# A mixture-of-experts kernel without a last stage: every expert block gathers its rows' sums, adds, normalises and scatters

## The chip, the cores and the metric

The kernel runs on one core of a Trainium2 chip. The metric is the device time of one execution in microseconds (us). The names of the engines: PE is TensorE, with its weight loads as PEld, DVE is VectorE, ACT is ScalarE, POOL is GpSimd, SP is SyncE. DMAs issued by an engine's queue are written SPq or ACTq; those of POOL are rows of POOL itself.

## The reference

One layer of a streaming encoder. After attention and a recurrence, every token (2048 of a prompt, 128 of running streams) goes through two of 32 SwiGLU experts, the result is added to its residual row, and the row is normalised:

```
t = rmsnorm(y, norm2_w)                      # 2176 rows of 1024
experts, gates = router(t)                   # 2 of 32 experts for each token
# rows sorted by expert, in blocks of 128 rows of one expert
for each block:  ys = (silu(xb @ wg[e]) * (xb @ wu[e])) @ wd[e]      # 1024 -> 512 -> 1024
y = y + segment_sum(ys * gate, row_token)    # each token gets two rows
y_prompt, y_sample = rmsnorm(y, final_w)
```

All of it is float32. The other outputs (keys, values, states) are written by earlier stages and are not touched.

## The kernel before

The program is a row of stages, each closed by a barrier of all engines: `project`, `attend_sample`, `attend_mix`, `experts`, `finish`. When `experts` starts, DRAM holds `h2` (the normalised rows) and `y` (the residual rows), and SBUF holds lists of which token each row of each block is.

`experts` works on 45 blocks of 128 rows, block b with expert `run_of(b)`. Some experts have one block and some have two (a run of blocks). There is no scheduler: each engine has its own program, the order of which is written out by hand, and semaphores tie them. For block b:

- **SP** loads the three weight matrices of an expert (2 MB each) into one of two slots, as soon as the block that used the slot last is through with it.
- **POOL** gathers the 128 token rows (`gather`, four indirect DMAs, 3 blocks ahead), the gates (`gate_of`), and at the end scatters the block's result (`scatter`): an indirect DMA that adds `block_out` to the rows of `scratch_y` in DRAM. Two scatters must not overlap, since two blocks can hold the same token, so each waits for the one before it (`o_out`).
- **PE** runs `gate_up(b)` (`gate_psum` L1968, `up_psum` L1972) and then `down(b - 1)` (`down_psum` L1983), 16 matmuls of 128x512 each.
- **ACT** takes exp of the gate (L1867), then issues 16 small DMAs (`spread_a`, L1874) that lay `hidden` out for the transpose, then empties the first half of `down_psum` of the block before (`copy_out`, L1880).
- **DVE** runs, in this order: `hidden(b)` (L1911 to L1917), `turn_x(b + 1)` (L1906), `copy_out(b - 1)` (the other half of `down_psum`, L1929), `turn_a(b)` (the transpose that makes `hidden_T`, L1922, once the 16 DMAs have landed). `down(b)` needs `hidden_T`, and `gate_up(b + 1)` needs `turn_x(b + 1)` and `hidden(b)`.

`finish` then loads the 17 tiles of `scratch_y` by SP, takes the mean square on ACT (L2047 to L2049), scales on DVE (L2057), and stores the tiles into two output tensors. The first load of `finish` can start only after the last scatter has landed and the barrier is past.

## Time and profile before

| | |
|---|---|
| median of 3 runs | 2894.78 us (2892.29 to 2896.38) |
| the profiled execution | 2889.87 us, span 2888.1 us |
| PE busy in the span | 2686.8 us (93%) |
| DVE, ACT, POOL busy | 1494.0 us (52%), 720.3 us (25%), 664.2 us (23%) |
| expert blocks | from about 1877 us to 2823 us |
| from the last `down_psum` to the end of the span | 2823.1 us to 2888.1 us |
| bytes moved by DMA | 404.42 MB |

The span runs from the first to the last recorded event; the device time is 1.8 us longer. PE is busy nearly all the time up to the last expert block, and not at all in `finish`.

### The profile page before, as it was taken

To read this page: it belongs to the slowest core of one execution; us is meant where nothing else is said; L and a number is where in the kernel's file an instruction comes from. 1 tells how busy PE (TensorE), PEld (TensorE's weight loads), DVE (VectorE), ACT (ScalarE), POOL (GpSimd) and SP (SyncE) were. 2 spreads that over 40 slices of the span, in tenths; PEclk is the share of its full clock that TensorE was granted. 3 is DMA by queue.
4 is the path that set the end of the run, shared out by engine and by line. 5 is a ranking of instruction groups with operands and counts; after the bars stand their busy time and mean duration, and the time that the engine had idled before them with its cause. 6 is when DMAs were issued, how large, how long until landed. Compare 5 with 4: busy or idle time off the path is not lost. (4 is left out here: it accounts for less than half of the span.)

```text
span 2888.1 us, 38265 instructions
## 1 busy us (share of the span) xinstructions
PE 2686.8 (93%) x11801; PEld 1617.9 (56%) x11802; DVE 1494.0 (52%) x2787; ACT 720.3 (25%) x2014; POOL 664.2 (23%) x921
## 2 busy tenths in 40 slices
PE   8999999999999986999999999499999999999990
PEld 6777777777777765555555555244444444444430
DVE  2565655556655564676777775434343434343333
ACT  1222222122222213555556664000000000000004
POOL 2111111111111111112222222223233333333330
PEclk9999999999999997999999999599999999999995
DMA  6010001000010046322121212299888688886877
GB/s 249 31 36 26 25 25 40 29 33 25 25 36 33 26 135 239 117 88 79 53 88 45 66 63 78 77 374 308 299 266 279 198 280 277 288 278 211 268 236 269
DMA packets 225977, 404.42 MB, mean 140 GB/s; under 512 B 30866, under 2 KB 88594, under 8 KB 225888
## 3 DMA queue, kind: packets, MB, share of 16 engines
q1 hardware_dynamic: 172976, 342.30, 33.4%
q0 software_dynamic: 18208, 48.64, 6.7%
q10 hardware_dynamic: 34704, 12.37, 1.7%
q8 instruction: 46, 0.75, 0.1%
q14 instruction: 43, 0.35, 0.0%
HBM read 310.62 MB, written 80.79 MB: 136 GB/s over the span
## 5 line engine op out<-in xcount | busy, mean ns | idle before, releaser
L670 PE MATMUL z_psum<-w_in_sb,hT 128*128 128x512 f32 x1088 | 480.5, 592 | 0.0
L664 PE MATMUL z_psum<-hT,w_in_sb 128*128 128x128 f32 x3264 | 375.2, 276 | 3.0 <-DMA w_in_sb<-in_w_in 3.0
L664 PEld LDWEIGHTS z_psum<-hT,w_in_sb 128*128 128x128 f32 x3264 | 371.0, 193 | 3.8 <-issue 3.8
L1968 PE MATMUL gate_psum<-w_gate_sb,block_rows_T 128*128 x720 | 321.4, 600 | 20.4 <-DMA w_gate_sb<-in_w_e_gate 20.4
L1983 PE MATMUL down_psum<-w_down_sb,hidden_T 128*128 x720 | 318.2, 595 | 7.1 <-DVE hidden_T L1922 7.1
L670 PEld LDWEIGHTS z_psum<-w_in_sb,hT 128*128 128x128 f32 x1088 | 200.5, 190 | 221.0 <-issue 221.0
L1972 PE MATMUL up_psum<-w_up_sb,block_rows_T 128*128 x720 | 316.3, 592 | 0.0
L1636 PE MATMUL y_psum<-w_out_sb,mix_T 128*128 128x512 f32 x512 | 239.7, 612 | 11.2 <-DVE mix_T L1391 11.2
L1265 ACT ACTIVATE w_in_sb<-score_psum,neg_max 128x512 f32<-128x512 f32 (+3 forms) x320 | 196.8, 622 | 209.5 <-DVE neg_max L1352 209.3
L1968 PEld LDWEIGHTS gate_psum<-w_gate_sb,block_rows_T 128*128 128x128 f32 x720 | 138.5, 193 | 195.9 <-issue 195.9
L1983 PEld LDWEIGHTS down_psum<-w_down_sb,hidden_T 128*128 128x128 f32 x720 | 137.4, 191 | 180.8 <-issue 180.8
L310 POOL TENSOR_TENSOR level_decay<-log_decay 128x256 f32<-128x256 f32 x116 | 73.5, 634 | 704.4 <-DVE level_operand L505 704.4
L1972 PEld LDWEIGHTS up_psum<-w_up_sb,block_rows_T 128*128 128x128 f32 x720 | 136.8, 190 | 172.2 <-issue 172.2
L1880 ACT ACTIVATE block_out<-down_psum,block_gates 128x512 f32<-128x512 f32 x45 | 30.9, 687 | 805.3 <-issue 795.0
L1215 POOL TENSOR_SCALAR w_in_sb<-w_in_sb,seg_factor,map_coef 128x512 f32<-128x512 f32 (+3 forms) x160 | 112.2, 711 | 493.5 <-DVE seg_factor L1365 493.5
L1352 DVE TENSOR_REDUCE neg_max<-score_psum 128x2 f32<-128x1024 f32 (+3 forms) x160 | 170.1, 1063 | 91.8 <-PE score_psum L1599 88.8
L1922 DVE STREAM_TRANSPOSE hidden_T<-hidden_by_lane 128x512 f32<-128x512 f32 x45 | 32.0, 711 | 348.3 <-DMA hidden_by_lane<-hidden 348.3
L1816 POOL DMA_INDIRECT block_rows<-scratch_h,block_tokens x188 | 179.4, 954 | 80.4 <-issue 41.1
L1834 POOL DMA_INDIRECT scratch_y<-block_out,block_out_rows x45 | 73.5, 1634 | 496.6 <-ACT block_out L1880 492.3
L1636 PEld LDWEIGHTS y_psum<-w_out_sb,mix_T 128*128 128x128 f32 x512 | 93.6, 192 | 149.2 <-issue 126.5
L1618 PEld LDWEIGHTS att_out_psum<-w_in_sb,weights_T 128*128 128x128 f32 x1088 | 133.5, 192 | 72.8 <-issue 61.0
L520 DVE COPY_PREDICATED scores_T<-level_mask,level_psum 128x512 f32<-128x512 uint8 x133 | 97.5, 733 | 146.8 <-PE level_psum L685 146.8
(295 smaller groups left out, 3389.7 us busy)
## 6 DMA issues: line engine op xcount, KB each, us to landing
w_gate_sb<-in_w_e_gate SPq DMA_DIRECT2D x32, 2048.0 KB, 13.8
w_up_sb<-in_w_e_up SPq DMA_DIRECT2D x32, 2048.0 KB, 13.3
w_down_sb<-in_w_e_down SPq DMA_DIRECT2D x32, 2048.0 KB, 15.0
w_in_sb<-in_w_in SPq DMA_DIRECT2D x7, 2048.0 KB, 19.1
hidden_by_lane<-hidden ACTq DMA_DIRECT2D x720, 16.0 KB
scratch_z<-z_ring SPq DMA_DIRECT2D x34, 256.0 KB, 2.0
scratch_y<-w_in_sb SPq DMA_DIRECT2D x17, 512.0 KB, 2.6
scratch_h<-h SPq DMA_DIRECT2D x17, 512.0 KB, 2.6
```

Source lines behind the costliest of these rows:

```text
L520: ins = nc.vector.copy_predicated(heads(A[:, :]), mk, heads(lps[pos % 2][:, :]))
L664: mm = pe.matmul(out[:, hd * P:(hd + 1) * P], w[:, g, c, hd * P:(hd + 1) * P], hT[:, u, c, :], start=(c == 0), stop=(c == DC - 1))
L670: mm = pe.matmul(out[:, :], hT[:, u, c, :], w[:, g, c, :], start=(c == 0), stop=(c == DC - 1))
L1215: pool.tensor_scalar(w1, w1, fac[:, u % 2, 1, s:s + 1], coef[:, 1:2], ALU.mult, ALU.mult).then_inc(w1_ok, 1)
L1265: ins = nc.scalar.activation(pr, sps[n % 2][:, c, 0:kw * P], ACT.Exp, bias=nmax[:, u % 2, c, s:s + 1], accum_out=zsum[:, u % 2, c, s:s + 1])
L1352: red(nmax[:, u % 2, :, s:s + 1], sps[n % 2][:, :, 0:kw * P], AX.X, ALU.max, negate=True).then_inc(m_ok, 1)
L1618: mm = pe.matmul(ops[:, 0:P], wT[:, n % 2, b * P:(b + 1) * P], v[:, k0 + b, head(u)], start=(s == 0 and b == 0), stop=(s == count(u) - 1 a ...
L1636: mm = pe.matmul(bank(m, part)[:, :], mT[:, m % 2, c, :], wo[:, c, part * HW:(part + 1) * HW], start=(c == 0), stop=(c == DC - 1))
L1816: pool.indirect_dma_start(out=xg[:, u, i, :], out_offset=None, in_=dr["h2"].rearrange("t (j d) -> (t j) d", j=LANES), in_offset=bass.Indir ...
L1968: mm = pe.matmul(gps[:, :], xT[:, u, c, :], part(wg, slot, c), start=(c == 0), stop=(c == DC - 1))
L1972: mm = pe.matmul(ups[:, :], xT[:, u, c, :], part(wu, slot, c), start=(c == 0), stop=(c == DC - 1))
L1983: mm = pe.matmul(dps[:, half, :], aT[:, u, c, :], part(wd, slot, c, slice(half * HW, (half + 1) * HW)), start=(c == 0), stop=(c == FC - 1))
```

## The change

`finish` is gone. `experts` now makes the sums and the finished rows itself:

- POOL: `sums(b)` gathers the block's rows of `scratch_y` into `block_sums`, after the scatter of the block before has landed. `scatter(b)` writes the new sums back as a plain write, without adding. `final(b)` scatters the normalised rows into a new output array `out_y_all`, that holds the prompt's rows, the streams' rows and 128 rows of padding, and is cut in two by views on the host. A token's row is written twice, and the second write, which holds the full sum, stays. The last block has no `scatter` and no `gate_of`.
- DVE: `copy_out` becomes `add` (two instructions, one for each half of `down_psum`, that scale by the gate and add `block_sums`), and `final` (one instruction over 1024 columns) comes after `turn_a`.
- ACT: `copy_out` is gone. `stats` takes the mean square of the sums and its root's inverse, after `spread_a`. A load of the activation table stands at the head of the loop's body, which is two blocks long, and ahead of and behind the loop.
- PE: the matmuls are the same; `down` waits for `add` where it waited for the two copies.

```diff
-            def scatter(b, u):
+            def sums(b, u, finals):
                 wait(pool, o_out, 16 * b)
+                wait(pool, f_out[u], 16 * finals)
                 pool.tensor_copy(dest[:, u:u + 1], col(tok_all, b)).then_inc(dest_ok, 1)
                 pool.wait_ge(dest_ok, b + 1)
-                pool.wait_ge(d_act, b + 1)
-                pool.wait_ge(d_dve, b + 1)
+                pool.sem_inc(stand, 1)
+                pool.indirect_dma_start(out=yg[:, u, :], out_offset=None, in_=dr["y"],
+                                        in_offset=bass.IndirectOffsetOnAxis(ap=dest[:, u:u + 1], axis=0)).then_inc(y_in, 16)
+            def scatter(b, u):
+                pool.wait_ge(s_ok, b + 1)
                 pool.sem_inc(stand, 1)
                 pool.indirect_dma_start(out=dr["y"], out_offset=bass.IndirectOffsetOnAxis(ap=dest[:, u:u + 1], axis=0),
-                                        in_=out[:, u, :], in_offset=None, compute_op=ALU.add).then_inc(o_out, 16)
+                                        in_=out[:, u, :], in_offset=None).then_inc(o_out, 16)
                 gate_of(b + 2, u)
+            def final(b, u, finals):
+                pool.wait_ge(f_ok, b + 2)
+                wait(pool, f_out[1 - u], 16 * finals)
+                pool.sem_inc(stand, 1)
+                pool.indirect_dma_start(out=dr["y_all"], out_offset=bass.IndirectOffsetOnAxis(ap=dest[:, u:u + 1], axis=0),
+                                        in_=fo[:, u, :], in_offset=None).then_inc(f_out[u], 16)
...
             with pool.Fori(1, n) as i:
                 gather(i * 2 + 3, 1)
+                sums(i * 2, 0, i)
+                final(i * 2 - 1, 1, i)
                 scatter(i * 2, 0)
                 gather(i * 2 + 4, 0)
+                sums(i * 2 + 1, 1, i)
+                final(i * 2, 0, i)
                 scatter(i * 2 + 1, 1)
-            scatter(n * 2, 0)
+            sums(n * 2, 0, n)
+            final(n * 2 - 1, 1, n)
+            final(n * 2, 0, n)
...
-            def copy_out(b, u):
...
-                nc.scalar.activation(out[:, u, 0:HW], dps[:, 0, :], ACT.Copy, scale=gcol[:, u:u + 1]).then_inc(d_act, 1)
+            def stats(b, u):
+                act.wait_ge(s_ok, b + 1)
+                wait(act, f_ok, b)
+                chain.after(nc.scalar.activation(junk[:, :], out[:, u, :], ACT.Square, accum_out=st[:, u, 0:1]))
+                chain.after(nc.scalar.activation(st[:, u, 1:2], st[:, u, 0:1], ACT.Ln, scale=1.0 / D, bias=consts["eps"][:, 0:1]))
+                nc.scalar.activation(st[:, u, 2:3], st[:, u, 1:2], ACT.Exp, scale=-0.5).then_inc(r_ok, 1)
...
             with act.Fori(1, n) as i:
+                nc.scalar.preload_act_table_set(ACT_SET)
                 blk(i * 2 + 1, 1)
...
-                ts(out[:, u, HW:D], dps[:, 1, :], gcol[:, u:u + 1], None, ALU.mult).then_inc(d_dve, 1)
+            def add(b, u):
                 dve.wait_ge(d_ps, b + 2)
...
+                dve.wait_ge(y_in, 16 * b + 16)
+                wait(dve, r_ok, b)
+                for half in range(2):
+                    c = slice(half * HW, (half + 1) * HW)
+                    ins = nc.vector.scalar_tensor_tensor(out=out[:, u, c], in0=dps[:, half, :], scalar=gcol[:, u:u + 1], in1=yg[:, u, c],
+                                                         op0=ALU.mult, op1=ALU.add)
+                ins.then_inc(s_ok, 1)
+            def final(b, u, finals):
+                dve.wait_ge(r_ok, b + 2)
+                wait(dve, f_out[u], 16 * finals)
+                nc.vector.scalar_tensor_tensor(out=fo[:, u, :], in0=out[:, u, :], scalar=st[:, u, 2:3], in1=fw[:, :],
+                                               op0=ALU.mult, op1=ALU.mult).then_inc(f_ok, 1)
...
                 hidden(b)
                 turn_x(b + 1, 1 - u)
-                copy_out(b - 1, 1 - u)
+                add(b - 1, 1 - u)
                 turn_a(b, u)
+                final(b - 1, 1 - u, finals)
...
-def finish(nc, dr, consts):
```

How this moves instructions: on DVE, the first of the two blocks in the loop's body, from the transpose of the gathered rows to the gate's first step of the next block, in the kernel before:

```order
L1906 STREAM_TRANSPOSE block_rows_T<-block_rows 128x1024
L90 REGISTER_ALU
L1928 ISA
L1929 TENSOR_SCALAR block_out<-down_psum,block_gates 128x512
L1920 REGISTER_ALU
L1922 STREAM_TRANSPOSE hidden_T<-hidden_by_lane 128x512
L1911 TENSOR_SCALAR silu_gate<-silu_gate 128x512
```

and in the changed kernel:

```order
L1944 STREAM_TRANSPOSE block_rows_T<-block_rows 128x1024
L1965 ISA
L1966 ISA
L1970 SCALAR_TENSOR_TENSOR block_out<-down_psum,block_gates,block_sums 128x512 x2
L1958 REGISTER_ALU
L1960 STREAM_TRANSPOSE hidden_T<-hidden_by_lane 128x512
L90 REGISTER_ALU
L1979 SCALAR_TENSOR_TENSOR block_final<-block_out,final_stats,final_row 128x1024
L1949 TENSOR_SCALAR silu_gate<-silu_gate 128x512
```

The one instruction over `down_psum` became two, and a third stands between the transpose of `hidden_by_lane` and the next block's `hidden`.

On POOL, one block in the loop's body, from the gathers of token rows to the gates, before:

```order
L1812 COPY block_tokens<-block_rows_all 128x4
L1813 REGISTER_ALU
L1816 DMA block_rows<-scratch_h,block_tokens 128x256 x4
L90 REGISTER_ALU
L1829 ISA
L1829 COPY block_out_rows<-block_tokens_all 128x1
L1834 DMA scratch_y<-block_out,block_out_rows 2304x1024
L1820 REGISTER_ALU
L1820 COPY block_slots<-block_slots_all 128x1
L1823 DMA block_gates<-scratch_gates,block_slots 128x1
```

and now:

```order
L1817 COPY block_tokens<-block_rows_all 128x4
L1818 REGISTER_ALU
L1821 DMA block_rows<-scratch_h,block_tokens 128x256 x4
L90 REGISTER_ALU
L1835 ISA
L1835 COPY block_out_rows<-block_tokens_all 128x1
L1838 DMA block_sums<-scratch_y,block_out_rows 128x1024
L1852 DMA out_y_all<-block_final,block_out_rows 2304x1024
L1844 DMA scratch_y<-block_out,block_out_rows 2304x1024
L1825 REGISTER_ALU
L1825 COPY block_slots<-block_slots_all 128x1
L1828 DMA block_gates<-scratch_gates,block_slots 128x1
```

Two indirect DMAs were put ahead of the scatter: the gather of this block's sums and the scatter of the finished rows of the block before.

## Rows read from the trace of the kernel before

**Rows 1.** Windows: stretch, us, busy PE, PEld, DVE, ACT, POOL, PEclk, DMA share, GB/s.

```profile
1900.00:2823.00 923.00, 915.90 (x2126) 404.71 (x2125) 339.10 (x309) 56.28 (x88) 307.30 (x391) 0.99 0.83 270
2840.00:2888.10 48.10, 0.00 (x0) 0.00 (x0) 21.66 (x17) 28.29 (x69) 0.00 (x0) 0.50 0.96 382
```

**Rows 2.** Waits, 1870 to 2830 us: who waited for whom: us, times, longest.

```profile
PE down_psum L1983 <- DVE hidden_T L1922: 7.1, 1, 7.1
POOL block_out_rows L1829 <- DMA scratch_y<-block_out,block_out_rows: 19.5, 14, 3.2
```

**Rows 3.** Timeline of a block with weights in flight: start, us, engine, line, what.

```profile
2033.86 0.71 DVE L1922 STREAM_TRANSPOSE hidden_T<-hidden_by_lane 128x512 f32<-128x512 f32 x1 [8.60 <-DMA hidden_by_lane<-hidden]
...
2037.89 7.03 PE L1983 MATMUL down_psum<-w_down_sb,hidden_T 128*128 x16
...
2039.21 0.69 DVE L1917 TENSOR_TENSOR hidden<-up_psum,silu_gate 128x512 f32<-128x512 f32 x1 [0.22 <-DVE silu_gate L1913]
2039.82 1.23 DVE L1906 STREAM_TRANSPOSE block_rows_T<-block_rows 128x1024 f32<-128x1024 f32 x1
2039.94 10.14 ACTq L1874 DMA_DIRECT2D hidden_by_lane<-hidden  x16
...
2044.76 7.03 PE L1968 MATMUL gate_psum<-w_gate_sb,block_rows_T 128*128 x16
...
2054.80 0.71 DVE L1922 STREAM_TRANSPOSE hidden_T<-hidden_by_lane 128x512 f32<-128x512 f32 x1 [8.90 <-DMA hidden_by_lane<-hidden]
...
2058.49 7.03 PE L1983 MATMUL down_psum<-w_down_sb,hidden_T 128*128 x16
```

**Rows 4.** Timeline of the stage's first down, and of a block whose weights are there.

```profile
1921.15 7.03 PE L1968 MATMUL gate_psum<-w_gate_sb,block_rows_T 128*128 x16
...
1932.00 0.71 DVE L1922 STREAM_TRANSPOSE hidden_T<-hidden_by_lane 128x512 f32<-128x512 f32 x1 [9.89 <-DMA hidden_by_lane<-hidden]
...
2321.59 0.71 DVE L1922 STREAM_TRANSPOSE hidden_T<-hidden_by_lane 128x512 f32<-128x512 f32 x1 [7.92 <-DMA hidden_by_lane<-hidden]
...
2327.67 10.14 ACTq L1874 DMA_DIRECT2D hidden_by_lane<-hidden  x16
...
2339.04 0.71 DVE L1922 STREAM_TRANSPOSE hidden_T<-hidden_by_lane 128x512 f32<-128x512 f32 x1 [4.74 <-DMA hidden_by_lane<-hidden]
```

**Rows 5.** Windows one block wide, of each kind (columns as in rows 1).

```profile
2032.10:2052.70 20.60, 20.60 (x49) 9.12 (x48) 7.66 (x7) 1.28 (x2) 6.62 (x10) 1.00 1.05 359
...
2320.50:2341.10 20.60, 20.60 (x49) 9.12 (x48) 8.63 (x9) 1.28 (x2) 6.80 (x9) 1.00 0.40 115
```

**Rows 6.** Timeline of POOL: two scatters, and the next copy of row numbers.

```profile
2093.70 1.62 POOL L1834 DMA_INDIRECT scratch_y<-block_out,block_out_rows  x1 [11.48 <-ACT block_out L1880]
...
2104.73 0.18 POOL L1829 COPY block_out_rows<-block_tokens_all 128x1 uint32 x1 [1.69 <-DMA scratch_y<-block_out,block_out_rows]
...
2813.79 1.63 POOL L1834 DMA_INDIRECT scratch_y<-block_out,block_out_rows  x1 [10.61 <-ACT block_out L1880]
...
2820.54 0.18 POOL L1829 COPY block_out_rows<-block_tokens_all 128x1 uint32 x1 [3.15 <-DMA scratch_y<-block_out,block_out_rows]
```

**Rows 7.** Timeline of the last block and of the last stage.

```profile
2813.36 0.71 DVE L1922 STREAM_TRANSPOSE hidden_T<-hidden_by_lane 128x512 f32<-128x512 f32 x1 [5.29 <-DMA hidden_by_lane<-hidden]
...
2823.35 0.75 DVE L1929 TENSOR_SCALAR block_out<-down_psum,block_gates 128x512 f32<-128x512 f32 x1 [9.28 <-PE down_psum L1983]
2825.01 1.61 POOL L1834 DMA_INDIRECT scratch_y<-block_out,block_out_rows  x1 [4.29 <-DVE block_out L1929]
...
2840.42 1.28 ACT L2044 ACT_TABLE_LOAD   x1 [16.41 <-PEq L72]
2845.69 1.06 ACT L2047 ACTIVATE square_out<-y_final 128x1024 bf16<-128x1024 f32 x1 [4.00 <-DMA y_final<-scratch_y]
...
2847.53 1.28 DVE L2057 SCALAR_TENSOR_TENSOR y_out<-y_final,final_stats,final_row 128x1024 f32<-128x1024 f32 x1 [23.43 <-ACT final_stats L2049]
...
2883.71 0.33 SPq L2034 DMA_DIRECT2D out_y_sample<-y_out  x1
```

More of the change, by code:

```diff
@@ L1842, in _ @@
             gather(2, 0)
+            sums(0, 0, 0)
             gather(3, 1)
@@ L1845, in _ @@
             gather(4, 0)
+            sums(1, 1, 0)
+            final(0, 0, 0)
             scatter(1, 1)
@@ L1861, in _ @@
             n = load(act, trips[0:1, 0:1], 1, MAXT)
+            chain = Chain(act, act_step)
             def gate(b):
```

106 lines of the change are left out of this document (35 added, 71 removed).

## The prediction, made before the changed kernel was run

> **What bounds the kernel now.** I read the windows first, to see which engine has no room. Over the expert blocks PE is busy 915.9 of 923 us at a granted clock of 0.99, and in the last stage it has nothing to do, while the DMA moves 382 GB/s for 48.1 us [rows 1]. So there are two limits. In the expert stage it is PE: one block is 2058.49 - 2037.89 = 20.60 us from `down` to `down` [rows 3]. In the last stage it is the DMA. Then the waits: `down` waits once for `hidden_T`, 7.1 us [rows 2], at the last block. The question is what disappears behind the last `down`, and whether anything added to DVE, ACT, POOL and the DMA breaks the cover that PE gives.
>
> The third view is the timeline of one block, read as a ring. DVE makes `hidden`, ACT issues 16 DMAs, they land, DVE transposes them to `hidden_T`, and only then does DVE start the next `hidden`. With weights in flight one transpose starts 2054.80 - 2033.86 = 20.94 us after the other [rows 3]: 5.35 to L1917, 0.73 to the first issue, 10.14 of issues, 4.72 of landing. Where the weights are there already, the landing is 2339.04 - 2337.81 = 1.2 us and the step 17.45 us [rows 4]. So **a second ring, of nearly PE's length, lies right behind PE's**: 0.3 us slower than PE in a loaded block, 3.2 faster in a quiet one. Of the 45 windows of one block between 1867 and 2794 us I count 14 with a DMA share of 0.39 to 0.70, the others at 0.96 to 1.05, as the two of [rows 5]: 14 quiet blocks, and behind the first one 29 loaded steps.
>
> Where the ring stands against PE is one number, x: the start of `hidden_T` counted from the end of the `down` before it, which is the start of the `gate_psum` matmuls. In the loaded block of [rows 3] x is 2054.80 - 2044.76 = 10.0 us.
>
> **What goes.** The last `down` is read at 2823.35 and the span ends at 2888.1 [rows 7]: 64.75 us. In the changed kernel this tail is as follows. `add` is two instructions; for one half there are 0.75 (from PSUM) and 0.64 (half of L2057's 1.28), and I take 0.72, so 1.45 us. 0.1 to ACT. From the start of L2047 to the start of L2057, 2847.53 - 2845.69 = 1.84. The scaling, 1.28. Then POOL picks it up after 0.91 (from DVE's end at 2824.10 to 2825.01) [rows 7], and the scatter lands 6.75 us after its issue, as the one at 2813.79 did, with no weights in flight [rows 6]. With the start at 2823.35 the sum ends at 2835.7, if `down` ends when it does now. **Gain 52.4 us.** Bounds of the landing: at most 4.4 us, for a plain store issued at 2883.71 [rows 7], and 11.03 us, for a scatter beside weights [rows 6]: gain 48 to 55. The sums of the last block must be there in time; their gather starts when scatter 43 has landed, which by 6.75 us is some 6 us ahead of the last `down`'s end. I count it as hidden.
>
> **What comes, engine by engine.**
>
> PE: nothing. `down` waits for `add`, which ends some 1.6 us after the `down` before it and is needed 13.7 us after it (two thirds of 20.60).
>
> ACT loses its copy and gets `stats`, 1.8 us, and at the head of each second block a table load of 1.28 [rows 7]. Its DMA issues are out at x - 4.7 in a loaded block, so the next exp can start at x - 1.6, ahead of DVE, which comes for it at x + 2.0. In a quiet block it starts at x + 1.9, about half a us late, in at most 4 of the 14: 2 us, left out. The Trainium skill (ScalarE: Activation LUTs, What ACT_TABLE_LOAD costs) puts a drain of about 1.38 us behind the load at a switch to another set; with it those 4 blocks would cost some 6 us more. The trace shows the load alone, 1.28, and the set here is the one in use.
>
> DVE: `add` costs 0.7 us more than the copy, at a place where DVE waits 4.7 us and more for the DMAs [rows 3, 4]: hidden. **`final`, 1.28 and 0.02 to start, is not hidden.** It stands between the transpose and the next `hidden`, inside the ring. A loaded step becomes 20.94 + 1.30 = 22.24, 1.64 over PE's 20.60, and a quiet one 17.45 + 1.30 = 18.75, 1.85 under it.
>
> The ring meets PE where PE needs `turn_x(b + 1)`: it ends 5.35 + 1.30 + 0.61 + 1.23 = 8.5 us after the start of the transpose, and PE comes for it at 20.6, so the limit is x = 12.1. (`down` itself would wait from x = 13.0.) The first block of the stage has x = 1932.00 - 1921.15 = 10.9 [rows 4], so the limit is reached in the next step. From there each loaded step over the limit is lost to PE, and a quiet one gives 1.85 of room. The room never gets so large that x would fall to where PE holds it now, so the account is one line: 29 x 1.64 = 47.6, less 14 x 1.85 = 25.9, plus what x has fallen at the end, 10.9 - 10.25 = 0.7: **22.4 us lost**. The last block pays once more: its `down` has no `gate_up` ahead of it and waits for `hidden_T`. There x is 6.2 now (5.29 of idle time [rows 7], behind a copy that takes 0.75 and starts 0.2 after `down`), and 10.25 then: 4.0 us. **Loss 26.4 us.**
>
> The ends of this term: with a landing 0.5 us shorter in loaded blocks it is 29 x 0.5 less, 12; with one 0.5 longer, 41. I stay with the landing of today's rows, which is that of the same DMAs beside the same weights.
>
> POOL gets two more indirect DMAs of 1.62 for each block. It waits 10.6 and 11.5 us ahead of a scatter today [rows 6], so its time is covered. New is a **chain through DRAM**: scatter(b - 1), its landing, sums(b), its landing, add(b), scatter(b). From a scatter to the next copy of row numbers POOL needs 11.03 - 1.69 = 9.34 us for its own work [rows 6]; then 1.0 to the gather's issue, g for its landing, 0.1 to DVE, 1.45 for `add`, 0.9 to POOL: 12.8 + g. The trace has no gather of this size. The bounds for g are 6.75 and 11.03 us, both of adding scatters of the same rows [rows 6]: 19.5 to 23.8 us against PE's 20.6. Only 14 of 45 scatters landed later than 9.34 us [rows 2], so I take 8: 20.8 us, on a par with PE and shorter than the ring. And `add` can be some 5 us late before the transpose behind it is.
>
> DMA: a loaded block moves 359 GB/s x 20.6 us = 7.4 MB [rows 5]. Two transfers of 0.52 MB more make 8.4, less what the adding scatter read. At the 382 GB/s of the last stage [rows 1] that takes 22.1 us, about the ring's 22.2: it doesn't add to it, but it says that loaded blocks stay loaded.
>
> **Sum.** Gain 52.4, loss 26.4, net 26.0 us. The profiled execution, 2889.87 us, becomes 2863.9; it is 4.9 us below the median of the runs, so the median of 2894.78 becomes 2868.8. Forecast **2869 us**.
>
> **Rivals.**
>
> 1. *The ring keeps its room.* The landing shrinks, since a plain scatter is shorter than an adding one, or since the weights come at a slower pace with PE. Then the loss is 0 to 12 us, and the time 2894.8 - 52.4 + 6 = 2848. For it: the term hangs on 1.64 us a step, of which half a us of landing takes a third. Against it: in the loaded blocks the DMA share is 1.05 [rows 5], with nothing to spare.
>
> 2. *The quiet blocks stop being quiet.* With x near 12 the last of the 16 DMAs in a quiet block is issued about 9 us after `down`, close to where the next expert's weights may start. Then a quiet step gives nothing back, or even costs what a loaded one does: 47.6 us, up to 47.6 + 14 x 1.64 = 71, and 4 at the end. Time 2894 to 2917; I take 2900, slower or the same. For it: the landing goes from 1.2 to 4.7 us when weights are in flight [rows 3, 4]. The Trainium skill (DMA: Bandwidth & Descriptors, Queues, rings and completion order) says that a DMA engine goes from one queue to the next only after a whole packet of some 9 to 17 descriptors; by that rule the new gathers and scatters would lengthen this landing as well, and the time would be that of this rival. No row here shows such a transfer beside the 16 small ones.
>
> 3. *The chain through DRAM becomes the bound*, place: DVE's wait for the sums. With g at 11.03 in 30 blocks and 6.75 in the others it costs 30 x 3.2 - 14 x 1.1 = 81 us: 2894.8 - 52.4 + 81 = 2923, slower than before. It decides from 44 x (12.8 + g - 20.6) > 52.4, a mean g over 9.0 us. For it: the 11.03. Against it: that was an adding scatter, and most were under 9.34.
>
> 4. *The tail doesn't shrink as it should*, since the close of the program has a cost of its own. The span holds 4.4 us behind the last store [rows 7], and the device time 1.8 behind the span: some us at most, inside the range.
>
> **Chances.** Forecast (loss 12 to 45, so 2854 to 2887): 0.50. Rival 1: 0.22. Rival 2: 0.13. Rival 3: 0.15. A measurement of this kernel tells about 0.2%, 5.8 us. Faster by more than that: 0.50 + 0.22 + 0.03 = 0.75. Within it: 0.10, out of rivals 2 and 3. Slower: 0.15. The range goes from a loss of 4 us, 2846, into rival 2, 2897; 0.05 is left out below and 0.15 above.
>
> **What would show it.** In the profile after: a span that ends 12 to 13 us behind the last `down`, with no SPq rows there. In the expert stage PE waits, 1 to 2 us each, for `block_rows_T` or `hidden_T` by DVE, in the rows of loaded blocks and not around quiet ones, and from `hidden_T` to `hidden_T` it is 22.2 us there. If DVE's `add` waits 5 us and more for the gathered sums, it is rival 3; if the distance is 22 us also where the weights are there, rival 2; if PE has no waits, rival 1. I am wrong altogether if PE's waits name `add`, or the weights.

## The result

The changed kernel is slower: 2927.43 us (median of 4 runs, 2922.29 to 2932.77) against 2895.58 before (4 runs, beside it on the same chip), a ratio of 1.0111 with a 95% interval of 1.009 to 1.0133. Forecast were 2869 us and a range from 2846 to 2897. The profiled execution took 2929.27 us, its span 2927.5.

The medians differ by 32 us, the two profiled executions by 39.4: the one before lies 5.7 under its median, this one 1.8 over. Sums from the traces, here and below, are to be set against the 39.4. The first fence holds the timeline of the changed kernel from the last `down` to the end (start, us, engine, line, what, idle time before it):

```profile
2912.01 1.41 DVE L1970 SCALAR_TENSOR_TENSOR block_out<-down_psum,block_gates,block_sums 128x512 f32<-128x512 f32 x2 [8.57 <-PE down_psum L2036]
2913.45 1.06 ACT L1909 ACTIVATE square_out<-block_out 128x1024 bf16<-128x1024 f32 x1 [11.56 <-DVE block_out L1970]
...
2915.29 1.28 DVE L1979 SCALAR_TENSOR_TENSOR block_final<-block_out,final_stats,final_row 128x1024 f32<-128x1024 f32 x1 [1.87 <-ACT final_stats L1911]
2917.44 0.96 POOL L1852 DMA_INDIRECT out_y_all<-block_final,block_out_rows  x1 [12.14 <-DVE block_final L1979]
```

The last stage is gone: 2927.5 - 2912.01 = 15.5 us are left of the 64.75 of [rows 7], a gain of 49.3. But the last `down` is read at 2912.01, not at 2823.35: **the expert stage is 88.7 us longer** (88.7 - 49.3 = 39.4). Its waits in the changed kernel (1870 to 2925 us; who waited for whom: us, times, longest), which answer to [rows 2]:

```profile
DVE hidden_T L1960 <- DMA hidden_by_lane<-hidden: 558.5, 45, 15.9
PE down_psum L2036 <- DVE hidden_T L1960: 55.7, 29, 13.0
PE gate_psum L2022 <- DVE block_rows_T L1944: 32.6, 31, 16.7
DVE block_out L1970 <- DMA block_sums<-scratch_y,block_out_rows: 0.4, 1, 0.4
```

PE waits 55.7 us for the transpose that ends the ring, once 7.1 us before, and 32.6 for `turn_x`, which comes behind the ring's `hidden`; 16.7 of these are the start of the stage. The gathered sums are waited for once, 0.4 us. Windows of the same 800 us, before and then after (columns as in [rows 1]):

```profile
1900.00:2700.00 800.00, 800.00 (x1861) 353.96 (x1861) 299.22 (x272) 49.18 (x77) 268.70 (x342) 1.00 0.84 276
```

```profile
1900.00:2700.00 800.00, 752.82 (x1709) 323.10 (x1709) 329.29 (x314) 99.87 (x193) 290.57 (x384) 0.99 0.84 302
```

PE had no idle time and now has 47 us. The granted clock is nearly the same, and the DMA engines are no busier than before (0.84), though they move more. The page's chain of work that ended last is the ring's through this stage:

```profile
ACTq 14%; DVE 9%; DMA 9%; issue 2%; PE 1%; DVEq 0%; SPq 0%; POOL 0%; ACT 0%; POOLq 0%
ACTq L1903 14%; DMA hidden_by_lane<-hidden 8%; DVE silu_gate L1950 5%; DVE block_final L1979 2%; DMA w_gate_sb<-in_w_e_gate 1%; DVE hidden L1955 1%; DVE silu_gate L1951 1%; DVE silu_gate L1949 1%; PE down_psum L2036 0%; PE gate_psum L2022 0
```

**The ring in three terms.** From the starts of the rows of `hidden` and `hidden_T` in all 45 blocks I worked out for each run: r, from the transpose `hidden_T` to the next `hidden`; 10.87, which is 0.73 to the first issue and 10.14 of 16 issues [rows 3]; and the landing, what then is left to the next transpose. Their sum is the step by construction, in every run, so it proves nothing by agreeing; it says which part of the step grew. Where DVE waits for PE, that wait lies in r. Since 10.87 is held fixed, a train of issues that takes longer than 10.14 us counts as landing (in the mean it took 10.17 before and 10.32 after). Before, the mean landing is 3.66 us, 14 of 45 are under 2 us (the quiet blocks), and the step is PE's, 20.51. After:

6.54 + 10.87 + 5.15 = 22.56 us, against a mean step of 22.53 (45 landings, 44 steps).

44 steps of 2.02 us more are 89, the stage's whole loss. With the landing of before it would be 6.54 + 10.87 + 3.66 = 21.07, and 44 x 0.56 = 25 us. So `final` in the ring is some 25 us, near the forecast, and **64 us come from a landing that is 1.5 us longer: no landing is under 2 us any more**.

**Which landings.** Set beside the same block of the kernel before, 59 of the 64 us lie in its 14 quiet blocks, where the mean landing rose from 1.23 to 5.45 us. In the other 31 it went from 4.83 to 5.00.

Why, the trace shows in such a block, the 32nd. Its rows before, and then after (timeline):

```profile
2533.80 10.14 ACTq L1874 DMA_DIRECT2D hidden_by_lane<-hidden  x16
2539.15 7.03 PE L1968 MATMUL gate_psum<-w_gate_sb,block_rows_T 128*128 x16
2545.17 0.71 DVE L1922 STREAM_TRANSPOSE hidden_T<-hidden_by_lane 128x512 f32<-128x512 f32 x1 [4.87 <-DMA hidden_by_lane<-hidden]
2546.60 0.39 SPq L1778 DMA_DIRECT2D w_gate_sb<-in_w_e_gate  x1
```

```profile
2595.54 10.44 ACTq L1903 DMA_DIRECT2D hidden_by_lane<-hidden  x16
2597.66 7.03 PE L2022 MATMUL gate_psum<-w_gate_sb,block_rows_T 128*128 x16
2605.11 0.39 SPq L1783 DMA_DIRECT2D w_gate_sb<-in_w_e_gate  x1
2611.24 0.71 DVE L1960 STREAM_TRANSPOSE hidden_T<-hidden_by_lane 128x512 f32<-128x512 f32 x1 [11.71 <-DMA hidden_by_lane<-hidden]
```

SP's fetch of the next expert's `w_gate` waits for PE's last use of that slot, so it follows the block's `gate_psum`: 7.45 us behind their start in both kernels. The 16 small issues follow the ring. Before, they ended 4.8 us behind the start of `gate_psum`, and the weights came 2.7 us later, when all had landed. Now they end 8.3 us behind it, and **the weights are issued 0.9 us ahead of the last small transfer**. The queues' packets from 2606 to 2611.2 us there (queue, packets, MB, share of the engines), q1 the weights, q0 GpSimd's, q10 the 16 transfers:

```profile
q1 hardware_dynamic: 631, 1.29, 75.6%
q0 software_dynamic: 85, 0.25, 19.1%
q10 hardware_dynamic: 96, 0.03, 2.4%
```

It is the same in all 13 quiet blocks that have a fetch behind them (the 14th is the last block): in the changed kernel the weights are 0.4 to 1.7 us ahead of the last small issue and the landings, from its end on, 4.0 to 6.3 us; before, the weights were 0.1 us ahead in one block and 1.4 to 2.8 behind in 12, and every landing was 1.2 to 1.3.

It feeds itself. While PE has its own pace the 16 issues of a quiet block end early. Once PE waits for `turn_x`, `gate_psum` starts just behind it, and the last issue ends 10.87 us behind the start of `hidden`, less the 0.61 and 1.23 up to the end of `turn_x`: 9.0 us behind the start of `gate_psum` (measured, 7.9 to 9.2), past the 7.45 of the weights. So a ring that makes PE wait also takes from itself the quiet landings in which it would catch up.

GpSimd's transfers lie on some landings too. In the block before that one, which had weights in flight before the change (landing 4.8 us), the weights are now through early, and from 2584 to 2588.3 us there is this:

```profile
q0 software_dynamic: 250, 0.63, 44.8%
q10 hardware_dynamic: 448, 0.15, 13.5%
q1 hardware_dynamic: 8, 0.02, 1.2%
```

The landing is 2588.27 - 2585.84 = 2.4 us. In the quiet block of [rows 4], 2335 to 2339 us of the kernel before, the same view has one queue only, and the landing is 1.2 us:

```profile
q10 hardware_dynamic: 288, 0.10, 10.3%
```

The gathers are there because the change brings them forward without moving their lines. The timeline of GpSimd in that block of the changed kernel; its 16 issues began at 2575.70 and ended at 2585.84:

```profile
2578.93 0.96 POOL L1844 DMA_INDIRECT scratch_y<-block_out,block_out_rows  x1 [6.77 <-DVE block_out L1970]
...
2586.71 0.94 POOL L1821 DMA_INDIRECT block_rows<-scratch_h,block_tokens  x1 [0.30 <-issue]
```

Before, these gathers stood behind a scatter that waited for ScalarE's half of the copy, and ScalarE reached it behind its 16 issues: in one block ScalarE issued from 2595.94, copied at 2606.27, and GpSimd scattered at 2607.76. The change took ScalarE's half away, GpSimd waits for VectorE's `add` alone, and the whole of its work for the block goes out some 8 us earlier (3.2 us behind the first of the 16 issues here, 11.8 there), under the 16 transfers. So three things could make the ring long enough for PE to wait: 1.28 us in it, 1 MB a block more on the queues, and this move. The runs try them one by one.

### The profile page after: what moved, and what is told of

Same layout as the page of the kernel before. It is cut to its first block and busy times, and to the rows that moved or that the text cites. A ratio compares the mean times of both kernels' runs of the same rounds, so it can differ in the third digit from the quotient of the medians.

```text
span 2927.5 us, 38632 instructions
## 1 busy us (share of the span) xinstructions
PE 2707.5 (92%) x11801; PEld 1615.3 (55%) x11802; DVE 1551.8 (53%) x2860; ACT 763.6 (26%) x2103; POOL 718.7 (25%) x1008
## 5 line engine op out<-in xcount | busy, mean ns | idle before, releaser
L2036 PE MATMUL down_psum<-w_down_sb,hidden_T 128*128 x720 | 328.2, 610 | 55.7 <-DVE hidden_T L1960 55.7
L2022 PE MATMUL gate_psum<-w_gate_sb,block_rows_T 128*128 x720 | 323.6, 603 | 38.0 <-DVE block_rows_T L1944 32.6
L1909 ACT ACTIVATE square_out<-block_out 128x1024 bf16<-128x1024 f32 x45 | 47.5, 1057 | 873.7 <-issue 862.2
L1599 PE MATMUL score_psum<-w_in_sb,att_q 64*128 64x512 f32 (+3 forms) x640 | 162.2, 585 | 1.6 <-PEq L72 1.5
```

Source lines behind the costliest of these rows:

```text
L1599: mm = pe.matmul(sps[n % 2][:, c, 0:kw * P], q[r, p % 2, head(u)], k[r, k0:k0 + kw, head(u)], start=True, stop=True)
L2022: mm = pe.matmul(gps[:, :], xT[:, u, c, :], part(wg, slot, c), start=(c == 0), stop=(c == DC - 1))
L2036: mm = pe.matmul(dps[:, half, :], aT[:, u, c, :], part(wd, slot, c, slice(half * HW, (half + 1) * HW)), start=(c == 0), stop=(c == FC - 1))
```

## The experiments

Ratios are against the kernel before, on the same chip, with 95% intervals. Landing and step are means worked out as above; PE's pace is 20.5. "Overtaken" counts, of the 13 quiet blocks of the kernel before with a fetch behind them, those in which the weights are issued 0.4 us or more ahead of the last of the 16.

| run | us | ratio | r | landing | under 2 us | overtaken | step |
|---|---|---|---|---|---|---|---|
| before | 2895.58 | 1 | 6.00 | 3.66 | 14 | 0 | 20.51 |
| changed | 2927.43 | 1.0111 | 6.54 | 5.15 | 0 | 13 | 22.53 |
| e1_final_off_ring | 2889.45 | 0.9987 | 5.37 | 5.43 | 0 | 9 | 21.67 |
| e2_ring_alone | 2922.02 | 1.0104 | 6.55 | 3.85 | 11 | 6 | 21.25 |
| e3_dmas_alone | 2926.86 | 1.0111 | 5.35 | 5.12 | 1 | 12 | 21.34 |
| e4_ring_and_dmas | 2972.68 | 1.0274 | 6.55 | 5.02 | 1 | 13 | 22.41 |
| e6_gather_alone | 2895.18 | 1.001 | 5.94 | 3.73 | 13 | 0 | 20.52 |
| e7_scatter_alone | 2887.24 | 0.998 | 5.89 | 3.78 | 14 | 0 | 20.53 |
| e11_two_gathers | 2937.05 | 1.0146 | 5.36 | 5.30 | 1 | 12 | 21.53 |
| e14_dve_copies_both | 2943.03 | 1.0168 | 5.36 | 5.49 | 0 | 8 | 21.71 |
| e5_silu_ahead | 2845.76 | 0.984 | 1.33 | - | - | 0 | 20.57 |

In e5 the transpose does not wait for the landing, so there is none to read. Counted from the last issue itself, 5 landings of e14 are 1.7 to 2.0 us: its 16 issues took 10.5 us in the mean.

The last column but one orders what follows. Over the 15 kernels that leave the hidden row's steps in their place, these are 195 blocks. In the 130 that are overtaken the landing, from the last issue on, is 3.7 to 6.8 us. In the other 65 it is 1.2 to 3.6, but for two: the first quiet block of e3 and of e11, with 5.5 and 6.6 us. No run holds the weights back and changes nothing else, so this is read from the traces of all these edits, and was not tried by hand.

**First: ring, transfers, both.** e1_final_off_ring moves `final` in the changed kernel to where VectorE waits anyway:

```diff
                 turn_x(b + 1, 1 - u)
...
+                final(b - 2, u)
                 add(b - 1, 1 - u)
                 turn_a(b, u)
-                final(b - 1, 1 - u, finals)
...
```

> The changed kernel with one instruction moved: DVE's final(b - 1) no longer stands between the transpose of block b and the hidden of block b + 1, but one block later, behind turn_x(b + 2) and ahead of add(b), where DVE waits for the 16 DMAs. All DMAs stay. Theory A (the 1.28 us inside the ring is what breaks the cover, and the longer landings follow from the lateness that it causes): the step from hidden_T to hidden_T falls to at most 20.9 us, PE's waits in the stage go under 10 us, and the time is 2895.6 less the tail's gain of some 49, so 2845 to 2860. Theory B (the new gathers and scatters lengthen the landing of the 16 DMAs by themselves, from 4.7 to over 6 us): the step is the 22.55 us of the changed kernel less 1.24, 21.3, over PE's 20.6, and the time is 2870 to 2885.

Measured: 2889.45 us, ratio 0.9987 (0.9977 to 0.9997), 38 us under the changed kernel. r fell by 1.17, the landing stayed long (9 of 13 overtaken), and PE still waits 47.6 us for `hidden_T`. The place of `final` matters, and is not all. Both theories missed: the time lies 4 us over B's range and far over A's.

e2_ring_alone is the kernel before with a spare instruction of the size of `final` at its place:

```diff
                 copy_out(b - 1, 1 - u)
                 turn_a(b, u)
+                spare()
...
```

> The kernel before, with one more DVE instruction of 1024 columns (1.28 us, on tiles that nothing else uses) between turn_a(b) and hidden(b + 1), and no other change; the last stage is still there. Theory A, as in the forecast's account: 22.4 + 4.0 = 26 us over before, 2922, with a loaded landing of 4.7 us and a quiet one of 1.2. If lateness alone turns the quiet blocks loaded: 50 to 75 over before. Theory B: 26 at most, as the DMAs are unchanged.

Measured: 2922.02 us, 1.0104 (1.0085 to 1.0123), 28 us. The landing hardly changes in the mean, and 11 are under 2 us. But they are not the same 11: in 6 of the 13 quiet blocks the weights are 0.4 to 1.3 us ahead and the landing is 3.7 to 5.5 us, in the other 7 they are at most 0.2 ahead and it is 1.2 to 1.3, and 3 of the 11 lie in blocks that were loaded before, where the weights are through early. So lateness alone does overtake, here in half of the blocks. The 26 us of the account came out, but not by its terms: it had all quiet landings at 1.2.

e3_dmas_alone is the kernel before with both transfers of the change as spare ones:

```diff
                 pool.wait_ge(dest_ok, b + 1)
...
+                pool.indirect_dma_start(out=yg[:, u, :], in_=dr["y"], ...).then_inc(y_in, 16)
...
+                pool.indirect_dma_start(out=dr["spare"], in_=go[:, :], ...).then_inc(f_out, 16)
+                pool.wait_ge(y_in, 16 * b + 16)
                 pool.wait_ge(d_act, b + 1)
```

> The kernel before, with two more indirect DMAs on POOL for each block, of the size and at the place of those in the changed kernel: a gather of the block's rows of scratch_y and a plain scatter of a spare tile into a spare array. Neither is used; DVE, ACT and PE are as before. Theory A: the loaded landing rises by less than 0.4 us, and the time is within 6 us of before. Theory B: the loaded landing is 6 us and more, the loaded step over 22 us, and the time 20 to 45 us over before.

Measured: 2926.86 us, 1.0111 (1.0091 to 1.013), 33 us, theory B's time with a shorter landing than its 6 us. All of it is in the landing, and 12 of 13 blocks are overtaken. The first quiet block has a landing of 5.5 us with the weights only 0.1 us ahead, where the kernel before has 1.3: there the added transfers themselves lengthen it. The DMA engines are at 0.94, with PE at 781 of 800 us:

```profile
1900.00:2700.00 800.00, 781.29 (x1798) 339.27 (x1797) 283.49 (x259) 43.66 (x75) 325.25 (x396) 1.00 0.94 314
```

e4_ring_and_dmas has both additions.

> Both additions at once: the spare DVE instruction in the ring and the two spare DMAs for each block, on the kernel before. If the two causes only add, the loss is that of the two runs before together; if they amplify each other, it is more than the sum. For the changed kernel's loss in the expert stage, 88 us, both theories together need 80 to 90 us here, so 2975 to 2985.

Measured: 2972.68 us, 1.0274 (1.0256 to 1.0293), 79 us, 2 under the lower end expected, and more than 28 + 33. Alone, each has to use up first what the ring lacks to PE's pace: by the means of the table it is 5.36 + 10.87 + 3.66 = 19.9 us without waits for PE, 0.6 under 20.5 (an estimate). 79 less the tail's 49 is 30, near the changed kernel's 32.

**Second: which transfer?** e6_gather_alone and e7_scatter_alone are e3 with only one of its two transfers.

> The kernel before, with one more transfer a block: a gather of the block's 128 rows of the sums into a spare array (its content is not used), issued and landed before the block's scatter. Both spare transfers together cost 33 us (e3_dmas_alone). If any 0.5 MB a block beside the hidden row's 16 transfers lengthens their landing: 12 to 20 us, mean landing 4.3 to 4.6 us, about 2906 to 2914. If only a write (the plain scatter) does it, because it goes out where the loaded and the quiet blocks' transfers start: under 6 us here, and 27 and more in e7_scatter_alone. If the gather does it, since GpSimd now also waits for it before the scatter and so everything behind it is issued later: 25 us and more here.

> The kernel before, with one more transfer a block: a plain scatter of 128 rows of zeros into a spare array (read by nothing), issued just before the block's own scatter. If any 0.5 MB a block does it: 12 to 20 us, mean landing 4.3 to 4.6 us, about 2906 to 2914. If the write alone does it: 27 us and more (over 2920). If the gather alone does it: under 6 us.

Measured: e6 2895.18 us, 1.001 (0.9992 to 1.0027); e7 2887.24, 0.998 (0.9971 to 0.999). Each alone is free, with 13 and 14 quiet landings and no block overtaken. No theory on record fits both numbers. The ten runs of e6 spread over 19 us, from 2885.58 to 2904.96, and its trace is of one at the lower end, 2887.86: whether some of its runs were overtaken isn't known. e11_two_gathers asks if it takes a read and a write:

```diff
                 pool.indirect_dma_start(out=yg[:, u, :], in_=dr["y"], ...).then_inc(y_in, 16)
+                pool.indirect_dma_start(out=yh[:, u, :], in_=dr["y"], ...).then_inc(y_in, 16)
-                pool.wait_ge(y_in, 16 * b + 16)
+                pool.wait_ge(y_in, 32 * b + 32)
```

> The kernel before with two spare gathers of the block's sums, one behind the other, ahead of the block's scatter: the same 1 MB a block as in e3_dmas_alone, but reads only. If the amount decides (0.5 MB more a block still leaves pauses of the weights under the 16 transfers, 1 MB more leaves none): 20 to 40 us slower, mean landing near 5 us. If it needs a gather and a plain scatter together (a read and a write at once): within 8 us of the kernel before, 12 and more landings under 2 us.

Measured: 2937.05 us, 1.0146 (1.0129 to 1.0163), 41 us, one landing under 2 us, 12 of 13 overtaken. So **half a MB a block more is free here and a whole one is not**, with reads alone too. The edit has a second effect: GpSimd's scatter waits 258.2 us for the two gathers (28 times; 83.1 in e6 and 3.0 in e3), so what is behind it goes out later, and amount and place are not cleanly apart in it. The DMA shares over the same 800 us are 0.84 before, 0.91 with one gather and 0.94 with two.

Then the same question in the changed kernel: e9_no_final_scatter leaves the scatter of the finished rows out, e10_no_gather the gather of the sums (each block adds to zeros).

> The changed kernel without the scatter of the finished rows (the y outputs are not written), 0.5 MB a block less; the sums are gathered, added to, normalised and scattered as in the changed kernel. So far, beside the kernel before: gather alone +1, plain scatter alone -7, both together +33, the ring's 1.28 us alone +28, all of it +79. Theory A (the landing of the hidden row's 16 transfers lengthens from 3.7 to 5.1 us only when the queues carry both added transfers, as these four runs say; with one of them the pauses of the weights still meet the 16 transfers): the landing falls to 3.7 to 4.2 us, the step of the ring from 22.5 to 21.3, the time from 2927 to 2865 to 2885 (of it some 3 us at the end, where nothing lands after the last scatter of a finished row). Theory B (in the changed kernel it is where the transfers stand, the gather of the sums or the scatter under the 16 transfers, and not their number): one of e9 and e10_no_gather stays above 2910 and the other falls by 40 and more.

> The changed kernel without the gather of the sums (each block adds to zeros, so the sums and outputs are not the reference's), 0.5 MB a block less. Theory A: as e9_no_final_scatter, 2870 to 2890. Theory B: see there. Theory C (the path through DRAM from a block's sums scattered to the next block's gather costs time although the profile shows 0.4 us of waits for it): the gain here is larger than in e9_no_final_scatter by 10 us and more.

Measured: e9 2915.41 us, 1.0076 (1.0059 to 1.0093); e10 2920.37, 1.0077 (1.0059 to 1.0095); only 12 and 7 us under the changed kernel where 40 and more were expected, with landings of 4.72 and 5.01 us. By their ratios the two are alike. All theories missed. What keeps the landings long is the place of the weights: with `final` still in the ring PE still waits for it, and 10 and 11 of the 13 blocks are overtaken. In e9 the others have landings of 1.2 to 2.2 us. Nor does the path through DRAM cost anything that shows: e10 has none and gains no more than e9.

**Third: the place of GpSimd's work.** e14_dve_copies_both makes, in the kernel before, only the move of GpSimd's work:

```diff
@@ VectorE, copy_out
+                ts(out[:, u, 0:HW], dps[:, 0, :], gcol[:, u:u + 1], None, ALU.mult)
                 ts(out[:, u, HW:D], dps[:, 1, :], gcol[:, u:u + 1], None, ALU.mult).then_inc(d_dve, 1)
@@ ScalarE, copy_out: left out; GpSimd and TensorE no longer wait for it
-                pool.wait_ge(d_act, b + 1)
```

> The kernel before, with ScalarE's half of `copy_out` done on VectorE, behind its own half: nothing is added to the transfers and nothing to the ring (the copy stands ahead of turn_a, where VectorE waits for the landing anyway), but GpSimd's scatter and the gathers behind it no longer wait for ScalarE, whose copy stood behind the 16 transfers, and go out some 8 us earlier, under the landing. This is the move that the changed kernel made without a line of the diff naming it. Theory P: 15 to 35 us slower, under 5 landings below 2 us, GpSimd's queue at some 0.3 of the engines in the landing. Theory R: within 5 us of the kernel before.

Measured: 2943.03 us, 1.0168 (1.015 to 1.0186): **50 us for an edit that adds no byte and nothing to the ring**, more than theory P had allowed. The landing of the 31 loaded blocks rose from 4.83 to 5.67 us, the gathers being on it, and 8 of 13 quiet blocks are overtaken; in the other 5 it is 2.7 to 3.6. The timelines of GpSimd and of ScalarE in it, one block:

```profile
2619.20 1.63 POOL L1833 DMA_INDIRECT scratch_y<-block_out,block_out_rows  x1 [11.23 <-DVE block_out L1921]
...
2623.79 0.98 POOL L1816 DMA_INDIRECT block_rows<-scratch_h,block_tokens  x1 [0.79 <-POOL block_tokens L1812]
...
2627.58 0.94 POOL L1816 DMA_INDIRECT block_rows<-scratch_h,block_tokens  x1 [0.30 <-issue]
```

```profile
2614.71 10.60 ACTq L1873 DMA_DIRECT2D hidden_by_lane<-hidden  x16
```

and VectorE's transpose behind them:

```profile
2631.24 0.71 DVE L1913 STREAM_TRANSPOSE hidden_T<-hidden_by_lane 128x512 f32<-128x512 f32 x1 [12.86 <-DMA hidden_by_lane<-hidden]
```

The four gathers are issued from 2623.79 to 2628.52, around the end of the 16 issues at 2625.31, and the landing takes 5.9 us. PE waits 51.2 us for `hidden_T`, 30 times.

e13_scatter_late tries to undo the move in the changed kernel, e15_final_off_ring_late in e1 and e16_no_final_late in e9, all with one line:

```diff
             def scatter(b, u):
                 pool.wait_ge(s_ok, b + 1)
+                pool.wait_ge(r_ok, b + 2)
...
```

> The changed kernel, with one more wait: GpSimd's scatter of a block's sums also waits for ScalarE's `stats` of the block, which stands behind the 16 transfers on ScalarE's queue, as ScalarE's copy did in the kernel before. So the scatter, the gate's gather and the four gathers of rows behind it go out some 8 us later, as they did before, and no longer while the 16 transfers land. Theory P (place: in the changed kernel these gathers were moved under the landing; place, amount and ring each end the quiet landings, and together they cost little more than two of them): since ring and amount alone cost 79 us beside the kernel before (e4_ring_and_dmas) and the changed stage 88, 5 to 12 us faster than the changed kernel, 2915 to 2923. Theory Q (the place is the main part of the 88 us): 2900 or less. Theory R (the place does nothing): 2925 to 2930. The gather of the next block's sums is late here and may add some us of waits of `add`, which is not in the ring.

> e1_final_off_ring (2889) with the late scatter of e13_scatter_late: of the three costs only the amount is left, 33 us (e3_dmas_alone), less the tail's 49. Theory P: 2875 to 2882, 8 to 14 us under e1_final_off_ring. Theory R: as e1_final_off_ring, 2887 to 2892.

> e9_no_final_scatter (the finished rows are not scattered; 2915) with the late scatter of e13_scatter_late. Of the added transfers only the gather is left, which cost nothing in e6_gather_alone, and the place is as in the kernel before, so of the three costs only the ring's 28 us is left, less the tail's 49. Theory P: 2870 to 2885, quiet landings are back (over 8 under 2 us). Theory R (removing one transfer bought 12 us in e9 for another reason): 2905 and more.

Measured: e13 2923.95 us (1.0111, 1.0095 to 1.0128), e15 2897.43 (1.0017, 1.0007 to 1.0026), e16 2906.97 (1.0043, 1.0028 to 1.0057). e13 can't be told from the changed kernel (the same ratio), e15 is 8 us slower than e1, e16 8 us faster than e9. e15 missed both its theories, e16's time is that of R, with 4 landings under 2 us, and e13 lies between P and R. The waits of e13 show that this is no clean undoing:

```profile
DVE block_out L1971 <- DMA block_sums<-scratch_y,block_out_rows: 318.7, 44, 10.0
DVE hidden_T L1961 <- DMA hidden_by_lane<-hidden: 254.6, 45, 15.0
```

The gather of the next block's sums became late with the rest, `add` waits 318.7 us for it, and the next scatter moves again. The landings are 4.97, 5.39 and 4.55 us, and 13, 12 and 11 of 13 blocks are overtaken: making GpSimd late does not bring PE's pace back, so the weights stay ahead. The 64 us can't be shared out between ring, amount and move, as each of them alone makes PE wait and so loses quiet landings (6, 12 and 8 of 13). The bounds: e4, which lacks the move, already costs 79 of the 88.

**Fourth: give the ring slack.** e5_silu_ahead is e1 with three of the four steps of the hidden row, 4.5 us of VectorE, done for the next block ahead of the transpose:

```diff
...
-            def hidden(b):
+            def silu(b):
                 dve.wait_ge(eg_ok, b + 1)
                 chain.after(ts(sg[:, :], sg[:, :], 1.0, None, ALU.add))
                 chain.after(nc.vector.reciprocal(sg[:, :], sg[:, :]))
                 chain.after(tt(sg[:, :], gps[:, :], sg[:, :], ALU.mult))
+
+            def hidden(b):
...
+                final(b - 2, u)
+                add(b - 1, 1 - u)
+                silu(b + 1)
                 turn_a(b, u)
+                hidden(b + 1)
+                turn_x(b + 2, u)
...
```

> The changed kernel with two edits: `final` stands before `add` as in e1_final_off_ring, and the first three steps of the hidden row (add one, reciprocal, product with the gate; some 4.5 us of VectorE) are done for block b+1 before `turn_a` of block b, so that behind `turn_a` only the one product stands before the 16 transfers of the hidden row start. Nothing of the computation is left out. Theory A (the change loses time because the ring turn_a, hidden row, 16 transfers, landing, turn_a is longer than TensorE's work of a block, and both what stands in the ring and a landing of 5.1 instead of 3.7 us make it so): the ring falls from 22.5 to about 17 us, TensorE becomes the bound again at some 20.6 us a block, the last `down` ends near 2830, TensorE waits for hidden_T under 10 us (55.7 in the changed kernel), the mean landing stays near 5 us, and with the tail of 15.5 us the time is 2840 to 2860, faster than both kernels. Theory B (the added transfers cost time in another way too: they slow the weights or the rows that TensorE waits for, or the expert blocks' GpSimd chain): the waits move to the weights or to the rows, and the time stays over 2870.

Measured: **2845.76 us, ratio 0.984 (0.9824 to 0.9857)**, the fastest kernel here, 82 us under the changed one with the same transfers and the same arithmetic. The timeline of VectorE in it: `hidden` now starts 1.1 us behind the transpose, the transpose's wait is not for the DMA, and in all 13 blocks the weights are issued 3.1 to 3.5 us behind the last of the 16:

```profile
2576.23 0.71 DVE L1962 STREAM_TRANSPOSE hidden_T<-hidden_by_lane 128x512 f32<-128x512 f32 x1 [0.21 <-DVE silu_gate L1951]
2577.29 0.69 DVE L1957 TENSOR_TENSOR hidden<-up_psum,silu_gate 128x512 f32<-128x512 f32 x1 [0.34 <-PE up_psum L2032]
...
2579.05 1.24 DVE L1977 SCALAR_TENSOR_TENSOR block_final<-block_out,final_stats,final_row 128x1024 f32<-128x1024 f32 x1
```

Its window and its waits for the ring, against 47 us of idle PE and 55.7 of waits in the changed kernel:

```profile
1900.00:2700.00 800.00, 798.87 (x1853) 350.83 (x1853) 367.93 (x344) 110.22 (x210) 315.37 (x415) 1.00 0.89 325
```

```profile
PE down_psum L2042 <- DVE hidden_T L1962: 8.3, 3, 7.2
DVE hidden_T L1962 <- DMA hidden_by_lane<-hidden: 4.7, 1, 4.7
```

Its control, e8_before_silu_ahead, is the same move in the kernel before (VectorE waits there for GpSimd's copy of the row numbers instead of for the scatter):

> Control for e5_silu_ahead: the kernel before with the same move of the three steps of the hidden row ahead of `turn_a`, and nothing else. In the kernel before the ring (20.5 us) and TensorE's work (20.6 us) are about equal and TensorE waits only 7.1 us for hidden_T and some more for the weights. Theory A: nothing is to be had here beyond these waits, 2880 to 2894 (0 to 14 us faster), so that e5_silu_ahead beats it by the 49 us of the tail less some 5 us. Rival: the ring had bound the loaded blocks here as well, and the time falls below 2870; then half of the gain of e5_silu_ahead is no credit of the change.

Measured: 2887.62 us, 0.9982 (0.9973 to 0.9992), 6 us. Where PE was the bound the move buys next to nothing, so of e5's 48 us some 42 are the change's.

e12_silu_ahead_only leaves `final` in the ring:

> The changed kernel with only the three steps of the hidden row moved ahead of `turn_a`; `final` stays behind `turn_a`, in the ring. Theory A (only the length of the ring against TensorE's 20.6 us a block counts): the ring is about 18.5 us, still under TensorE's block, so 2843 to 2852, within 4 us of e5_silu_ahead. If `final` in that place costs in another way (it makes `turn_x` and the hidden row late for TensorE's own waits): 2855 and more.

Measured: 2852.97 us, 0.9855 (0.9839 to 0.9872), 7 us over e5, between the two theories (up to 2852, from 2855); PE waits 12.8 us for `hidden_T`, 13 times. So `final` costs 38 us in a ring without slack and 7 in one with it.

## Why the prediction was wrong

**The tail** was right in kind, a little too good: 15.5 us where 12.4 were taken, a gain of 49.3 inside the bounds 48 to 55. `add` 1.41 (1.45 taken), from `stats` to `final` 1.84 (1.84), `final` 1.28 (1.28). The last scatter is issued at 2917.44 and the span ends 10.06 us later: 6.75 was taken, from a scatter in mid-stage. The upper bound, 11.03, would have been nearer.

**The ring's 1.28 us** was right. r rose from 5.35 to 6.54, the account gave a loss of 26.4 us, and e2_ring_alone measures 28. That agreement is in part luck: in e2 6 of 13 quiet blocks gave no room, and 3 others were quiet in their place. PE's waits name `hidden_T` and `block_rows_T`, as foretold, but not only in loaded blocks.

**The step that failed** is the room that the quiet blocks were to give back, the term "less 14 x 1.85 = 25.9", and with it "I stay with the landing of today's rows, which is that of the same DMAs beside the same weights." For the 31 loaded blocks that held, 4.83 and then 5.00 us. In the 14 quiet ones the landing was 5.45 us and not 1.2, as the weights went out ahead of the last small transfer. By the measured means such a step is 6.54 + 10.87 + 5.45 = 22.86 us, 2.26 over PE's 20.60, so 14 of them cost 31.6 where the sum had a gain of 25.9: 57.5 of the 62.3 us that the stage's loss of 88.7 lies over the forecast 26.4. The upper end, 0.5 us in the loaded blocks, had 41.

Two other things it had in hand push the same way. It computed 22.1 us of DMA time for a loaded block against a ring of 22.2, and concluded "it doesn't add to it"; yet 1 MB a block more alone makes PE wait (e3, e11: 33 and 41 us). And for GpSimd it counted what is added and not what is moved: the scatter's wait for ScalarE is struck out by the diff, and what was queued behind it, six indirect DMAs a block with the scatter, came 8 us forward, onto the landing (e14: 50 us alone). That "its time is covered" held for GpSimd's own time and said nothing of its transfers.

**Rival 2**, quiet blocks that stop being quiet, at 0.13, is what happened, and by the mechanism that it named: "the last of the 16 DMAs in a quiet block is issued about 9 us after `down`, close to where the next expert's weights may start." Measured, it is issued 7.9 to 9.2 us after, and the weights start at 7.5. Its price was short, a loss of up to 75 us in the stage where 88.7 came: it took such a step for a loaded one of 22.24, where 22.86 was measured, and the loaded ones are 22.4. The trace agrees in kind with the rule cited there, from the Trainium skill (DMA: Bandwidth & Descriptors, Queues, rings and completion order), by which other queues' transfers would lengthen this landing: beside GpSimd's gathers it was 2.4 us, alone 1.2. But in the quiet blocks it is the weights that carry 56 to 88% of the engines during the landing, not the new gathers and scatters.

**Rival 3**, the chain through DRAM, did not occur: `add` waits 0.4 us for the gathered sums. **Rival 1** is excluded by the landings. The table load in every second block took 1.28 us, and no wait of the changed kernel names it.

**GpSimd**: the added indirect DMAs took 0.96 to 0.99 us each, not the 1.62 taken, which only the adding scatter needs. It changed nothing.

## What to carry to other kernels

Before adding to a kernel whose bound engine is full, write the longest ring beside it as a sum and ask for each term what could lengthen it; a ring as long as the bound's step has no room for anything. If the account counts on quiet stretches to catch up, ask what keeps them quiet: here an order of two issues on different engines, one tied to PE and one to the ring, that turns over as soon as PE waits. That is why 1.28 us of VectorE, 1 MB of transfers or an earlier issue each cost 28 to 50 us alone, and why taking one of them away again gave little. When a diff strikes out a wait, follow what was queued behind it: it will run earlier, and its transfers may land on someone else's. And if such a change has a sure gain elsewhere, make slack in the ring first: 4.5 us of work taken out of it turned a loss of 32 us into a gain of 43 (e12), and with `final` out of it too, of 48 (e5).

## What the runs showed of the hardware

- The landing of the 16 transfers of 16 KB behind their last issue was 1.2 us alone, 2.4 with GpSimd's gathers at 45% of the engines, 4.7 to 4.9 in most blocks with weights in flight before the change, and up to 7.6 in the changed kernel. In four such windows, alone, beside gathers and beside weights, a packet of these transfers took 26 to 27 ns (median): what grows lies between the packets, not in them.
- A load of weights (2 MB) issued 0.4 us or more ahead of the last of the 16 made this landing 3.7 us and more in 130 of 130 blocks. Issued later than that it left it at 1.2 to 3.6, two of 65 blocks excepted.
- 0.5 MB a block more on GpSimd's queue cost nothing (e6, e7), 1 MB more 33 and 41 us (e3, e11), with DMA shares of 0.91, 0.90 and 0.94, 0.94. That is a fact of this ring, which had 0.6 us to PE's pace, and not a threshold of the engines.
- GpSimd was busy 1.62 us with an adding scatter of 128 rows of 4 KB, and 0.96 to 0.99 with a plain scatter or a gather of the same rows.
- The last scatter of the program was followed by 10.06 us to the end of the span (10.1 in e5, from 2834.37 to 2844.5), 3.3 more than from a scatter's issue to the release of its waiter in mid-stage.
